# A mixer, 32-expert and RG-LRU block kernel: first block's work in another order, out-projections finished by token tile

## The reference, cut to what matters

```python
# first block
u = rmsnorm(x, g_attn)
c_q, c_kv, k_r, q_s, k_s, v_s = split(u @ w_in)        # 384, 256, 32, 512, 512, 512 columns
q  = rmsnorm(c_q, g_cq) @ w_uq                         # the latent norms
kv = rmsnorm(c_kv, g_ckv) @ w_ukv
o_m = softmax attention of q, kv (rope on 32 columns); o_s = stick-breaking attention of q_s, k_s, v_s
h = x + concat(rmsnorm(o_m), rmsnorm(o_s)) @ w_o       # the first out-projection
h = h + moe(rmsnorm(h, g_moe))                         # top 4 of 32 experts, 12.6 MB of weights each
h = h + sigmoid(rmsnorm(h) @ w_ple_gate) * (p @ w_ple_proj)
# second block
mix = concat(attention, gated linear recurrence) @ w_out   # the second out-projection
x = x + rmsnorm(mix, g_post_mix)
up = conv3(rmsnorm(x, g_pre_ffn) @ w_up)               # 22 groups of 256 columns
x = x + rmsnorm((gelu(c_g) * c_u) @ w_down, g_post_ffn)
```

## Time and profile before

| | |
|---|---|
| median of 3 runs | 1412.57 us (1411.61 to 1415.88) |
| the profiled execution, its own time | 1414.68 us |
| its span, first to last instruction | 1412.9 us (1.78 us lie around it) |
| mean granted TensorE clock | 0.985 |
| PE busy | 1285.8 us (91%) |
| DVE, ACT, POOL busy | 489.1, 400.7, 59.0 us |
| moved from HBM | 478.39 MB |

### The profile page before, as it was taken

The page is one execution under the profiler, slowest core; times in us unless marked ns, Lnnn a source line. Parts: engine busy times, 40 slices in busy tenths (PEclk is TensorE's granted clock), DMA queues, the critical chain, the costliest instruction groups (busy, mean ns, idle before and its releaser), DMA issues.

```text
span 1412.9 us, 16571 instructions
## 1 busy us (share of the span) xinstructions
PE 1285.8 (91%) x6969; PEld 738.8 (52%) x6969; DVE 489.1 (35%) x735; ACT 400.7 (28%) x641; POOL 59.0 (4%) x115
## 2 busy tenths in 40 slices
PE   7989999999999889988888888888888999899998
PEld 7878543333333333333333333333324898799986
DVE  5795412111211112111121111211113777777765
ACT  5674312100111001110010100101003756755554
POOL 4001000000000000000000000000000510000000
PEclk9998899999999999999999999999999999999999
DMA  9437699999999999999999999999999964355520
GB/s 341 166 125 293 228 383 428 430 425 429 427 426 429 427 429 427 427 428 428 426 428 428 427 428 428 427 427 429 427 427 374 264 222 142 126 182 184 189 103 30
DMA packets 78474, 480.79 MB, mean 340 GB/s; under 512 B 5504, under 2 KB 40475, under 8 KB 53568
## 3 DMA queue, kind: packets, MB, share of 16 engines
q1 hardware_dynamic: 75904, 474.76, 82.9%
q0 software_dynamic: 2496, 4.96, 1.6%
HBM read 478.39 MB, written 1.31 MB: 340 GB/s over the span
## 4 chain that ended last, share of the span: by engine, by line
PE 51%; DMA 40%; DVE 4%; ACT 3%; issue 1%; DVEq 0%; SPq 0%; ACTq 0%
DMA arena<-in_w_dn_dram 38%; PE ps L1937 23%; PE ps L2333 11%; PE ps L2293 10%; DMA ring<-in_w_dn_dram 2%; PE ps L2260 1%; PE ps L2349 1%; DVE W L1224 1%; PE ps L1945 1%; PE ps L2450 1%; ACT arena L898 0%; PE ps L2217 0%; ACT arena L947 0%; PE ps L2304 0%; ACT W L766 0%
## 5 line engine op out<-in xcount | busy, mean ns | idle before, releaser
L2293 PE MATMUL ps<-ring,arena 128*64 128x512 f32 x1392 | 315.3, 597 | 11.8 <-DMA ring<-in_w_gu_dram 11.8
L2293 PEld LDWEIGHTS ps<-ring,arena 128*64 128x64 f32 x1392 | 98.7, 137 | 207.9 <-issue 175.4
L1937 PE MATMUL ps<-X,W 128*128 128x256 f32 x1560 | 189.1, 283 | 2.0 <-DVE W L1230 1.7
L1937 PEld LDWEIGHTS ps<-X,W 128*128 128x128 f32 x1560 | 187.8, 192 | 3.1 <-DVE W L1230 2.2
L1573 DVE TENSOR_SCALAR arena<-ps 128x512 f32<-128x512 f32 x32 | 22.1, 692 | 478.3 <-PE ps L2293 478.3
L1937 PE MATMUL ps<-W,X 128*128 128x512 f32 (+2 forms) x780 | 172.7, 381 | 3.8 <-DVE W L1224 1.9
L1224 DVE TENSOR_TENSOR W<-ring,W 128x2048 fp32r<-128x2048 f32 (+2 forms) x64 | 144.9, 2265 | 75.3 <-ACT W L766 75.3
L2333 PE MATMUL ps<-ring,arena 128*64 128x512 f32 x648 | 145.9, 595 | 22.9 <-DMA ring<-in_w_dn_dram 22.9
L1937 PEld LDWEIGHTS ps<-W,X 128*128 128x128 f32 x780 | 142.1, 188 | 31.8 <-DVE W L1224 4.0
L2293 PE MATMUL ps<-arena 128*64 128x512 f32 x656 | 150.5, 601 | 0.0
L960 ACT ACTIVATE arena<-arena 128x512 f32<-128x512 f32 x32 | 20.2, 631 | 459.3 <-DVE arena L1573 459.3
(11 more groups left out here) (348 smaller groups left out, 996.6 us busy)
## 6 DMA issues: line engine op xcount, KB each, us to landing
ring<-in_w_gu_dram SPq DMA_DIRECT2D x87, 2048.0 KB, 22.4
ring<-in_w_dn_dram SPq DMA_DIRECT2D x40, 2048.0 KB, 24.9
arena<-in_w_gu_dram SPq DMA_DIRECT2D x39, 2048.0 KB, 20.6
arena<-in_w_dn_dram SPq DMA_DIRECT2D x23, 2048.0 KB, 25.6
ring<-in_w_up_dram SPq DMA_DIRECT2D x22, 1024.0 KB, 5.1
ring<-in_w_in_dram SPq DMA_DIRECT2D x15, 1024.0 KB, 12.9
ring<-in_w_down_dram SPq DMA_DIRECT2D x11, 1024.0 KB, 4.9
ring<-in_w_o_dram SPq DMA_DIRECT2D x4, 1024.0 KB, 5.0
```

Source lines behind the costliest of these rows:

```text
L1937: y = e.matmul(o, l, r, start=start and i == 0, stop=stop and i == 2)
L2293: y = e.matmul(ps[c * 64:c * 64 + 64, use[0], :], xs[:, k, c0:c0 + CAP], w[:, half * D + c * 512:half * D + (c + 1) * 512], start=False, s ...
```

## The change

It alters the order in which engines do the same work, with few instructions more or less:
- SP loads g_attn between the two tiles of x; PE transposes tile 0 of x into all four banks first, then g_attn, then tile 1.
- PE does the first latent bank's part of piece 4 ahead of `pair_scores`, the other three behind it; the bias row goes behind piece 6. The banks from U_a to U_hk are dealt anew.
- ACT: a table load for Ln and split(7) come ahead of both Ln; split(8) behind the latent rows' copies; split(11) ahead of the values' copies; split(13) and two of the six copies of weights ahead of the last Exp.
- DVE: `stick_above(0)` and the first scans move behind split(7) and the rows' copies, `stick_above(1)` ahead of piece 9. The latent rows are no longer multiplied (four instructions go); the factor is put on q's, k's and v's rows as they leave PSUM, by instructions that were there.
- Both out-projections: their last two pieces are done by banks, (0,0), (0,1), (1,0) of the first piece, then of the second, then both pieces for bank (1,1). In the first block h's tile 0 is transposed ahead of that last bank. The semaphore that tells piece 14 or 32 free is raised behind bank (1,1)'s part. ACT's rows_hi waits for piece 14.
- In the second block square_h(0) and its root come ahead of the last bank's squares, with DVE's part to match; the feed-forward norm gets semaphores of its own.

The core of the diff:

```diff
@@ banks
-        U_z0, U_z1 = takes(2), [takes(2) for _ in range(2)]
-        U_rb = take()
-        U_a = [takes(2) for _ in range(2)]
-        U_v = takes(2)
-        U_cT = takes(3)
+        U_a = [[take(5), None], [None, None]]
+        U_z0, U_z1 = [take(6), take(7)], [[take(0), take(1)], [take(2), take(3)]]
+        U_a[0][1], U_a[1] = take(4), [take(6), take(7)]
+        U_rb = take(3)
+        U_v = [take(0), take(1)]
+        U_cT = [take(b) for b in (2, 4, 5)]
...
+        pair14 = pair_free[14]
         pair_free[14] = BK.filled(U_gath[NE // 4 - 1, 3])
@@ ACT, sticks and latent rows
+            prime(ACT.Ln)
+            split(7)
             for i in range(2):
                 e.wait_ge(*marks[i])
                 e.activation(l_two[i], l_two[i], ACT.Ln, bias=1.0).then_inc(logs, 1)
-                split(7 + i)
...
+            split(8)
...
+                    e.wait_ge(*normed["c", 0])
+                    e.activation(qrow[:, t, c * 384:(c + 1) * 384], whole(U_uq[t][c], 384), ACT.Copy,
+                                 scale=rs[:, t:t + 1]).then_inc(taken[U_uq[t][c][0]], 1)
@@ ACT, mixer's end
-            for a in range(2):
-                e.wait_ge(sticks, 2 + a)
-                e.activation(pairs_of(L1, a), pairs_of(L1, a), ACT.Exp).then_inc(weights, 1)
+            e.wait_ge(sticks, 2)
+            e.activation(pairs_of(L1, 0), pairs_of(L1, 0), ACT.Exp).then_inc(weights, 1)
             split(13)
...
+            for g in range(2):
+                weights_in(g)
+            e.wait_ge(sticks, 3)
+            e.activation(pairs_of(L1, 1), pairs_of(L1, 1), ACT.Exp).then_inc(weights, 1)
+            for g in range(2, 6):
+                weights_in(g)
@@ ACT, second out-projection
             prime(ACT.Sqrt)
             split(34)
...
             square_rows("mix", 0, U_mix)
             root_rows("mix", 0)
-            square_rows("mix", 1, U_mix)
+            square_rows("mix", 1, U_mix, (0,))
+            square_h(0)
+            root(1, 2, D, ffn_squares["ffn", 0], ss[:, 0:1], done=ffn_roots.sem)
+            square_rows("mix", 1, U_mix, (1,))
             root_rows("mix", 1)
-            square_h(0)
-            root(1, 2, D, squares["ffn", 0], ss[:, 0:1])
@@ DVE, latent rows
-            over_root("c", 1, 0, 4)
-            for a, b_ in ((0, 384), (384, 640)):
-                for t in range(2):
-                    c = 2 * (a > 0) + t
-                    x = e.tensor_scalar(prow[:, t, a:b_], prow[:, t, a:b_], rs[:, c:c + 1], None, ALU.mult)
-            x.then_inc(normed.sem, 1)
+            summed = stick_scans(0, range(4, 8), above)
+            above = stick_above(1)
+            e.wait_ge(*roots["c", 1])
+            e.reciprocal(rs[:, 0:4], rs[:, 0:4]).then_inc(normed.sem, 1)
             split(9)
@@ PE
+            def rows_part(s, ks, t, n, uses, x_ready, last):
+                hi, lo = halved(s)
+                e.wait_ge(*lo_done(s))
+                use, c = uses[t][n], slice(n * 512, (n + 1) * 512)
+                for i, k in enumerate(ks):
+                    e.wait_ge(*x_ready(k))
+                    y = mm3(whole(use), [z[:, k, t * P:(t + 1) * P] for z in xin], (hi[:, i, c], lo[:, i, c]), False,
+                            last and k == ks[-1], True)
+                if last:
+                    y.then_inc(full[use[0]], 1)
+                return y
...
-            rows_in(32, (0, 1), 0, U_mix, xin, 4, 3, 512, 1024, mix_ready).then_inc(s_pair, 1)
-            rows_in(33, (2, 3), 0, U_mix, xin, 4, 3, 512, 1024, mix_ready, by_tile=True)
+            for t, n in ((0, 0), (0, 1), (1, 0)):
+                rows_part(32, (0, 1), t, n, U_mix, mix_ready, False)
+            for t, n in ((0, 0), (0, 1), (1, 0)):
+                rows_part(33, (2, 3), t, n, U_mix, mix_ready, True)
+            rows_part(32, (0, 1), 1, 1, U_mix, mix_ready, False).then_inc(s_pair, 1)
+            rows_part(33, (2, 3), 1, 1, U_mix, mix_ready, True)
```

More of the change, by code:

```diff
@@ L779, in parts, with root @@
                     x.then_inc(x_hi.sem, 1)
-            def root(n, c, size, last, src=None, bias=epsc):
+            def root(n, c, size, last, src=None, bias=epsc, done=roots.sem):
                 e.wait_ge(*last)
                 e.activation(rs[:, c:c + n], ss[:, c:c + n] if src is None else src, ACT.Sqrt, scale=1.0 / size,
-                             bias=bias).then_inc(roots.sem, 1)
+                             bias=bias).then_inc(done, 1)
             def half_mean(name, t):
@@ L1134, in _, with square_rows @@
             split(34)
-            def square_rows(name, t, uses):
-                for n in range(2):
+            def square_rows(name, t, uses, ns=range(2)):
+                for n in ns:
                     e.wait_ge(*BK.filled(uses[t][n]))
@@ L1157, in _ @@
             square_h(1)
-            root(1, 3, D, squares["ffn", 1], ss[:, 1:2])
+            root(1, 3, D, ffn_squares["ffn", 1], ss[:, 1:2], done=ffn_roots.sem)
             for t in range(2):
@@ L1375, in _ @@
             split(6)
-            above = stick_above(0)
             split(7)
@@ L1859, in _ @@
                 add_rows(0, n, U_mix)
-            gained_rows("mix", 1, U_mix, gmix)
+            gained("mix", 1, 0, U_mix, gmix)
+            e.wait_ge(*ffn_roots["ffn", 0])
+            e.reciprocal(rs[:, 2:3], rs[:, 2:3]).then_inc(s_r0, 1)
+            gained("mix", 1, 1, U_mix, gmix)
             over_root("mix", 1, 1, 1)
-            add_rows(1, 0, U_mix)
-            e.wait_ge(*roots["ffn", 0])
-            e.reciprocal(rs[:, 2:3], rs[:, 2:3]).then_inc(s_r0, 1)
-            add_rows(1, 1, U_mix)
+            for n in range(2):
+                add_rows(1, n, U_mix)
             hi, lo = halved(34)
@@ L1868, in _ @@
             e.tensor_tensor(lo[:, 0:4], loads[SPL[34]][0][:, 0:4], hi[:, 0:4].bitcast(F32), ALU.subtract)
-            over_root("ffn", 1, 3, 1)
+            e.wait_ge(*ffn_roots["ffn", 1])
+            step(e.reciprocal(rs[:, 3:4], rs[:, 3:4]))
+            e.wait_ge(*own.now())
             e.tensor_scalar(u[:, 1, :], h[:, 1, :], rs[:, 3:4], None, ALU.mult).then_inc(normed.sem, 1)
@@ L2083, in pair_scores, with a_rows @@
                             y.then_inc(full[x[0]], 1)
+            def a_rows(s, k, t, c):
+                hi, lo = halved(s)
+                a, b_ = ((0, 384), (384, 672))[c]
+                use, i = U_a[t][c], k - 3 * (s - 4)
+                if k == 0:
+                    claim(use)
+                y = mm3(whole(use, b_ - a), [z[:, k, t * P:(t + 1) * P] for z in xin], (hi[:, i, a:b_], lo[:, i, a:b_]),
+                        k == 0, k == KD - 1, True)
+                if k == KD - 1:
+                    y.then_inc(full[use[0]], 1)
+                return y
+            e.wait_ge(*lo_done(4))
+            for k in range(3):
+                a_rows(4, k, 0, 0)
             for x in U_qk:
@@ L2087, in _ @@
             pair_scores(qsT, ksT, U_z0, U_z1)
+            for t, c in ((0, 1), (1, 0), (1, 1)):
+                for k in range(3):
+                    y = a_rows(4, k, t, c)
+            y.then_inc(s_pair, 1)
+            for s, ks in ((5, range(3, 6)), (6, range(6, 8))):
+                e.wait_ge(*lo_done(s))
+                for k in ks:
+                    for t in range(2):
+                        for c in range(2):
+                            y = a_rows(s, k, t, c)
+                if s < 6:
+                    y.then_inc(s_pair, 1)
             claim(U_rb)
@@ L2110, in _ @@
             rows_in(8, (4, 5), 0, one_bank(U_v), xin, 0, 7, 512, 512)
-            e.wait_ge(*normed["c", 0])
+            for t in range(2):
+                for c in range(2):
+                    e.wait_ge(*BK.emptied(U_a[t][c]))
             for i in range(3):
@@ L2218, in bias @@
                              start=True, stop=False)
[L2221 to L2229 removed]
+            turned_rows(1, 0)
             e.wait_ge(s_wg, 1)
```

111 lines of the change are left out of this document (57 added, 54 removed).

## The result

The changed kernel takes 1418.03 us, the median of 8 runs (1417.69 to 1420.35), against 1412.85 us of 8 runs of the kernel before (1411.61 to 1416.02). The ratio is 1.0039, with an interval of 1.0030 to 1.0048: slower by 5.2 to 5.5 us, just past the 0.3% that the forecast called no change. The profiled execution took 1417.69 us with a span of 1416.0 us, which is only 3.1 us more than the span before (1412.9). Both numbers have to be explained, the 3.1 and the 5.2.

What follows compares the result with a forecast made beforehand. PE (51% of the chain) and DMA (40%, in the experts) bound the kernel. Terms -0.2 - 2.1 - 0.2 + 5.3 + 0.5 = +3.3 us gave 1418.0 us profiled, 1415.8 us as median; range 1410.0 to 1420.5.

Steps and rivals of the forecast that it cites:

- the likeliest case: Whole kernel: no change that can be told, on the slow side, +1.5 to +5 us; chance 0.48.
- the first account: Everything ahead of the experts' start at 155 us: start -0.2, mixer -2.1, first out-projection -0.2 us.
- Second out-projection, +5.3: Around 1210 us: ACT's split(34) waits longer for piece 32, delaying tile 0 and the feed-forward by 5.3 us.
- The first rival: Second out-projection: the wait for piece 32 is hidden, so -0.5 us there, 1409.6 us in all; chance 0.12.
- The clock at the feed-forward's start, +0.5: First matmuls of the feed-forward: PE's doubled gap ahead of the transposes costs 0.5 us through half clock.
- the second rival: Feed-forward starts at half clock, PE from 1224 us on: +4.5 instead of +0.5, 1419.9 us; chance 0.18.
- Start, -0.2: PE's first transposes: half run while g_attn and x's second tile are on their way, saving 0.2 us.
- Mixer, -2.1: In-projections to mixer's end: earlier split(7) and DVE copies start PE's last mixer stage 2.1 us sooner.
- the first two stretches: Half-clock stretches on PE at 109 to 118 and 147 to 156 us; no change counted for them.
- First out-projection, -0.2: First out-projection and router: tile 0's transposes go under the last matmuls, starting the experts 0.2 us sooner.
- The carry from the profiled execution to the median, -2.1: Whole kernel: profiled execution stood 2.1 us above its median, so 1418.0 us became 1415.8 us.
- Rival 4: Ahead of the experts: another engine or a late weight holds the mixer, no gain, +5.8, 1418.4 us; chance 0.08.

Runs made afterwards that it cites:

- e1: Changed kernel with the second out-projection as before, all else of the change kept: 1413.27 us, ratio 1.0003 to the kernel before.
- e2: Kernel before with only the second out-projection's part of the change: 1417.77 us, ratio 1.0037.
- e3: Changed kernel with ACT's split(34) moved behind the squares and roots, ahead of tile 0's scaling: 1414.08 us, ratio 1.0005 to the kernel before.
- e8: Changed kernel with 30 unread 128x512 matmuls in PE's gap ahead of the feed-forward's transposes: 1418.32 us, ratio 1.0045 to the kernel before.
- e4: Kernel before, unchanged, run again for another trace: 1413.41 us, ratio 1.0002.
- e6: Kernel before with only the start's new order (loads and transposes of x and g_attn): 1413.76 us, ratio 1.0006.
- e7: Kernel before with the mixer's and first out-projection's parts, old start and old second out-projection: 1411.41 us, ratio 0.9992.
- e12: e7 with two unread matmuls (512 and 256 columns) fitted to PE's gap ahead of the mixer's last stage: 1408.62 us, ratio 0.9957 to the kernel before.
- e5: Kernel before with only the first block's part from piece 4 to the mixer's end: 1413.94 us, ratio 1.0007.
- e10: Kernel before with only the first out-projection's part of the change: 1413.19 us, ratio 0.9999.
- e9: e7 with six unread 128x512 matmuls ahead of the mixer's last stage: 1412.19 us, ratio 0.9992 to the kernel before.
- e11: e5 with six unread 128x512 matmuls ahead of the mixer's last stage: 1413.05 us, ratio 1.0000 to the kernel before.

## Why the prediction was right, and where it was wrong

The side was right and the size was not: +3.3 us forecast, +5.2 measured, inside the range and just outside the band that the likeliest case named, which was "no change that can be told". The second out-projection was right in size and mechanism; what did not come is the first account, -2.5 us forecast and nothing that e1 can tell. Point by point:

1. **Second out-projection, +5.3: right.** The step said that split(34) waits for 66 of 72 matmuls and that everything of tile 0 stands behind it. The changed trace has the idle time (6.63 us on ACT, 8.08 on PE, 7.9 forecast), from the last matmul to the high parts it is 5.2 us more, e2 gives +4.4 to +5.2 us for this part alone, and e3 removes 3.9 to 4.8 us by moving one call. The first rival, that the wait is hidden, is refuted.

2. **The clock at the feed-forward's start, +0.5: too small in the profiled pair, not borne out beyond it.** In the pair it was 1.2 us (7.5 instead of 6.3 us for the 48 products), and the half-clock stretch reached 3.9 us into the feed-forward, the place that the second rival named; its 4.5 us did not come. But the 6.3 us are the lowest of the ten profiles with the old second out-projection: they take 6.3 to 8.7 us there, 7.9 on average, against 7.5, 7.4 and 7.6 in the changed kernel, e2 and e8. The doubled gap cost the feed-forward no clock that these profiles show. From the projection's last matmul to the end of the 48 products the ten take 16.6 us on average (15.0 to 17.4), so that the changed kernel's 21.4 are 4.8 us more, and not the 6.4 of the pair. By the Trainium skill ("TensorE: Matmul & The Clock Gate", "What's actually happening") activity lifts the throttle. e8 agrees in so far as filling the gap shortens the stretch (nearly 14 to 7 us), and shows that this is no gain while waits remain right ahead of the work that counts.

3. **Start, -0.2: wrong in sign.** The step said that tile 0 comes first "and PE has idle time for it". It has, but the first product waits for DVE anyway and came no sooner: 10.74 us, before 10.56. What changed is PE's rate behind it: from the first product to the factor row it took 14.1 us instead of 12.95, although the one wait in between is gone. Other executions with the old start show up to 13.8 there (e4), so part of this is the execution's. In e1, x's second tile was late too (PE's first product at 11.99 us). The price is 0.8 us on average over the profiles and 1.2 in e6's medians, neither beyond its scatter.

4. **Mixer, -2.1: right as an amount of work, wrong as time.** PE's last stage came 2.5 us sooner than before against the same row, by the path that was forecast: DVE's copies follow each other at 103.81 and 105.16 us, as walked. The step that failed is in the part on the clock, "I count nothing for the first two stretches", although it names the new gap ahead of that stage (1.8 us forecast, 1.29 measured). A stretch at half clock stood behind the gap in five of six profiles, and it costs 2.9 us, the difference between e7's 9.9 and e12's 6.9 us from the stage to the out-projection: where it comes, it takes the gain and a bit more. Filling the gap returned it (e12), and this is the one claim of mine on the first account that an experiment supports. How much of the missing 2.1 us the gap explains stays open. The old order has a stretch in three of five profiles too, which leaves some 0.7 us for the gap (an estimate, 2.9 times the difference of the two shares). By the mean granted clock of all runs e5 stands well below the kernel before beside it (0.9835 against 0.9863), e7 hardly (0.9858 against 0.9863), and e1 hardly (0.9854 against 0.9860).

5. **First out-projection, -0.2: right as far as can be told**, by e10's -0.3 (its interval holds -1.4 to +1.1 us) and by the stretch from its first matmul to the first expert's, 36.2 us against 36.4 in e4, at a like clock.

6. **The carry from the profiled execution to the median, -2.1: the assumption failed.** I took an execution that stood 2.1 us above its median and subtracted these 2.1 from the forecast too. But the excess had a place: the half-clock stretches of the earlier trace rows in the mixer's end and the router, missing or shorter in e4, and the 96 runs of the kernel before tie their time to the mean clock in the same way. The changed kernel's profile has the same two stretches, and yet its profiled execution (1417.69 us) is the fastest of its eight runs; it had no such excess over its median that could be taken off. Profile against profile the sum was good (+3.3 forecast, +3.0 measured), in part by luck: up to SP's first down weights it was 3.75 us less where 2.5 were forecast, behind the projection 6.4 more where 5.8 were, and the clock had a hand in both. Median against median it was two short.

Rival 4 gave the right number, 1418.4 us, for a reason that did not hold: no engine and no late weight held the mixer. What is left open: where the mixer's gain goes in e1 and e7, beyond what the clock accounts for; whether the start's loss is real; what decides between the executions of one kernel with the gap open; and whether the same filling would help at the router or, with the late split, ahead of the feed-forward, which was not tried.

## What to carry to other kernels

Before a conversion is put ahead of a reduction on the same engine, look up what it waits for in the *new* order: moving the last reader of a buffer from matmul 48 to matmul 66 held up work that had nothing to do with that buffer. A gain that leaves a new gap on TensorE ahead of a long chain of small matmuls has to be priced with the clock behind it (2.9 us here), and a filling of the gap's length, into a bank that is free, is a cheap trial. And where one profiled execution stands off its median, find the place of the difference before carrying it to the forecast.

## What was not expected of the hardware

- Behind a wait of 1.29 us on PE came about 7 to 10 us at half clock, beginning 0.7 to 2.5 us behind its end, in five profiles of six. With 1.3 us of dense work in its place (e12), or 5.2 us (e9, e11), none came in three profiles. The first profile of the kernel before has such a stretch behind a wait of 0.49 us, e4 with the same wait none.
- Two executions of the same kernel differed by 4 us at one place (155.52 and 159.57 us), by the clock: the earlier one was even 1.0 us behind at the factor row (24.52 and 23.51).
- At the start PE can run at about half its pace with the granted clock recorded as 1.00: e12's PE completes 6 matmuls of 256 columns per microsecond from 11 to 15 us and 10 to 11 afterwards, and most of the other profiles show the same for 2 to 6 us.
- A matmul of 128x512 with plain float32 operands took 0.87 us (e9: 5.23 us for six, from 104.01 to 109.24 us), against 0.23 with fp32r operands (e8: 6.96 us for thirty).
